# Query root norms kept per token and applied to the attention scores, key root norms spread by one matmul

## What is computed

```python
n = rms_norm(h, attn_norm_w[l])
proj = n @ w_in[l]
aq, ak, av, rq, rk, rv, rg = jnp.split(proj, split_at, axis=-1)
aq = rope(rms_norm(aq.reshape(B, S, ATTN_HEADS, HEAD_DIM), q_norm_w[l]), pos)
ak = rope(rms_norm(ak.reshape(B, S, ATTN_KV_HEADS, HEAD_DIM), k_norm_w[l]), pos)
...
y_attn = windowed_gqa_sink(aq, ak, av, attn_sink[l])
...
def windowed_gqa_sink(q, k, v, sink):
    ...
    s = jnp.einsum('bnqkgd,bnjkd->bnkgqj', qb, kb).astype(jnp.float32) * scale
    s = jnp.where(valid[None, :, None, None], s, NEG_INF)
    m = jnp.maximum(jnp.max(s, axis=-1, keepdims=True), sink_l)
    p = jnp.exp(s - m)
    p = p / (jnp.sum(p, axis=-1, keepdims=True) + jnp.exp(sink_l - m))
```

## Time and profile before

| what | value |
|---|---|
| median of 3 runs | 2899.54 us (2899.49 to 2899.75) |
| the profiled execution's own time | 2900.2 us |
| its span | 2898.4 us |
| mean granted clock of PE | 0.987 |
| DVE, ACT, POOL busy over the span | 1596.1, 902.5, 1333.3 us |
| PE busy from 0 to 72 us | 52.22 us |
| PE busy from 72 to 145 us | 65.04 us |
| PE busy from 145 to 217 us | 72.00 us |

### The profile page before, as it was taken

One profiled execution on the slowest core, in us unless ns is written; L12 is line 12 of the kernel. 1 busy time (PEld: TensorE's weight loads), 2 busy tenths in 40 slices (PEclk: granted clock), 3 DMA queues, 4 the chain that ended last, 5 costly groups with the idle time before them and its releaser, 6 DMA issues. The chain is left out here.

```text
span 2898.4 us, 37077 instructions
## 1 busy us (share of the span) xinstructions
PE 2778.3 (96%) x13968; PEld 2248.7 (78%) x13968; DVE 1596.1 (55%) x2447; ACT 902.5 (31%) x1759; POOL 1333.3 (46%) x1012
## 2 busy tenths in 40 slices
PE   7899989999999999999999899999899999999997
PEld 5677768778888888777766688878777788888886
DVE  5576775485555555542367742133368655555555
ACT  5444422232222222333334510121243332222222
POOL 3323232355666556543222235446614656566663
PEclk9999999999999999999999999999999999999998
DMA  3010101111111111131101011122201111111111
GB/s 123 30 36 30 37 20 73 51 44 51 52 58 59 44 55 51 48 116 37 37 30 38 28 39 51 54 113 66 66 23 44 48 59 55 48 55 52 59 51 66
DMA packets 71378, 151.97 MB, mean 52 GB/s; under 512 B 6449, under 2 KB 29361, under 8 KB 70065
## 3 DMA queue, kind: packets, MB, share of 16 engines
q1 hardware_dynamic: 64256, 123.76, 13.4%
q10 hardware_dynamic: 6960, 26.01, 2.3%
HBM read 141.36 MB, written 8.39 MB: 52 GB/s over the span
## 5 line engine op out<-in xcount | busy, mean ns | idle before, releaser
L612 POOL TENSOR_TENSOR WH<-WRAW,CST 128x512 fp32r<-128x512 f32 x204 | 229.7, 1126 | 895.0 <-PE PS L728 768.7
L726 PE MATMUL PS<-XH,WH 128*128 128x512 f32 x1248 | 512.1, 410 | 3.5 <-DVE XL L2040 2.8
L728 PE MATMUL PS<-XH,WL 128*128 128x512 f32 x1248 | 489.6, 392 | 0.0
L727 PE MATMUL PS<-XL,WH 128*128 128x512 f32 x1248 | 488.9, 392 | 0.0
L637 POOL TENSOR_TENSOR WL<-WRAW,WH 128x512 fp32r<-128x512 f32 x216 | 309.7, 1434 | 273.1 <-ACT WH L1668 272.1
L2460 DVE TENSOR_TENSOR H<-H,PS 128x512 f32<-128x512 f32 x352 | 236.2, 684 | 161.8 <-PE PS L1052 159.4
L726 PEld LDWEIGHTS PS<-XH,WH 128*128 128x128 f32 x1248 | 235.5, 189 | 84.1 <-issue 37.2
L1050 PE MATMUL PS<-HH,WH 128*128 128x512 f32 x704 | 275.8, 392 | 5.3 <-DVE HL L2394 5.3
L614 POOL TENSOR_TENSOR WL<-WRAW,WH 128x512 fp32r<-128x512 f32 x204 | 272.1, 1334 | 16.0
L1668 ACT ACTIVATE WH<-WRAW 128x512 fp32r<-128x512 f32 x204 | 129.0, 632 | 471.6 <-PE PS L1052 383.3
L1051 PE MATMUL PS<-HL,WH 128*128 128x512 f32 x704 | 275.3, 391 | 0.0
(11 more groups left out here) (328 smaller groups left out, 5028.5 us busy)
## 6 DMA issues: line engine op xcount, KB each, us to landing
WRAW<-ws SPq DMA_DIRECT2D x104, 512.0 KB, 3.4
WRAW<-ws SPq DMA_DIRECT2D x176, 256.0 KB, 2.6
RAWX<-ws SPq DMA_DIRECT2D x88, 256.0 KB, 2.6
H<-xT ACTq DMA_DIRECT2D x4, 1024.0 KB, 11.3
H<-xT ACTq DMA_DIRECT2D x2, 2048.0 KB, 9.8
h_spill<-H ACTq DMA_DIRECT2D x1, 4096.0 KB, 12.9
H<-h_spill ACTq DMA_DIRECT2D x4, 1024.0 KB, 8.3
outT<-H ACTq DMA_DIRECT2D x4, 1024.0 KB, 4.4
```

The lines of the kernel that those rows point to most:

```text
L612: pool.tensor_tensor(WH[:, j, c], WRAW[:, j, c], ONES[:, 0:1].to_broadcast((P, 512)), ALU.mult).then_inc(hi_split, 1)
L726: pe.matmul(out, WH[:, j, w], rh(kt), start=(n == 0), stop=False)
L727: pe.matmul(out, WH[:, j, w], rl(kt), start=False, stop=False)
L728: last = pe.matmul(out, WL[:, j, w], rh(kt), start=False, stop=(n == len(kts) - 1))
```

## The change

Four edits. The inverse roots of query heads stay per token in a new tile `RTQ` (128x64), and DVE writes `Q1` without them (a plain add); the roots and the factor 0.125 are applied elsewhere. The mask step is now one multiply-add per head: scores times the query's inverse root of this token, plus the mask. For keys the squares are summed by one matmul with `BD` as weights, so that the sum of a head stands on each of its channels for each of 512 tokens; ACT takes the root of 128x512 into `XX[:, 1024:1536]`, DVE inverts all of it and multiplies it in, with the 0.125. `spread1` and its places in the hook are gone. And `norm_spread(0, 0)` moves from tile 3 to tile 6. The whole diff:

```diff
--- before.py
+++ after.py
@@ -251,7 +251,8 @@
         WH = sb(ctx, "WH", [P, 2, 1024], F32R)
         WL = sb(ctx, "WL", [P, 2, 1024], F32R)
         VEC = sb(ctx, "VEC", [P, NVEC])
-        sb(ctx, "as_the_weights", [P, 40])
+        RTQ = sb(ctx, "RTQ", [P, 64])
+        sb(ctx, "as_the_weights", [P, 104])
         CST = sb(ctx, "CST", [P, NKEEP])
         ACC = sb(ctx, "ACC", [P, 2, HALF])
         SQ = sb(ctx, "SQ", [P, 2, HALF])
@@ -355,7 +356,7 @@
             "r_turned", "r_kz", "r_kv", "r_state", "r_qx", "r_in", "r_si", "r_out", "r_copied"))
         r_sq, r_sum, r_root, r_inv, r_spread, r_norm = map(sem, ("r_sq", "r_sum", "r_root", "r_inv", "r_spread", "r_norm"))
         gate_th, gated, turned_heads, rst_made = map(sem, ("gate_th", "gated", "turned_heads", "rst_made"))
-        head_inv, head_spread = map(sem, ("head_inv", "head_spread"))
+        head_inv = sem("head_inv")
 
 
         prod, w_sum, w_high, w_high0, w_low = map(sem, ("prod", "w_sum", "w_high", "w_high0", "w_low"))
@@ -398,6 +399,10 @@
         def prob(s):
 
             return XX[:, 768 * (s % 2):768 * (s % 2) + 768].rearrange("p (a b) -> p a b", a=2)
+
+        def query_norm(j, b, n):
+
+            return RTQ[:, 16 * j + 2 * b:16 * j + 2 * b + n]
 
 
         RST = [RG[:, 3, half(h)] for h in range(2)]
@@ -854,9 +859,12 @@
                         pe.wait_ge(m_free, nm.n)
                     else:
                         pe.wait_ge(rst_made, 2)
-                    for b in range(4):
-                        sq = XX[:, (g % 2) * HALF + b * P:(g % 2) * HALF + (b + 1) * P]
-                        last = pe.matmul(PS[:, MB, 2 * b:2 * b + 2], sq, BD[:, 0:P:64], start=True, stop=True)
+                    x = XX[:, (g % 2) * HALF:(g % 2 + 1) * HALF]
+                    if kind == "k":
+                        last = pe.matmul(PS[:, MB], BD, x, start=True, stop=True)
+                    else:
+                        for b in range(4):
+                            last = pe.matmul(PS[:, MB, 2 * b:2 * b + 2], x[:, blk(b)], BD[:, 0:P:64], start=True, stop=True)
                     last.then_inc(m_full, 1)
                     nm.n += 1
                 elif kind == "v":
@@ -870,24 +878,12 @@
             def first_norm(h, kt):
                 if (h, kt) == (1, 0):
                     norm_sums(0, 0)
-                if (h, kt) == (1, 3):
+                if (h, kt) == (1, 6):
                     norm_spread(0, 0)
-
-            def spread1(g):
-
-                pe.wait_ge(head_inv, g + 1)
-                if g:
-                    pe.wait_ge(proj_done, g)
-                for b in range(4):
-                    for hh in range(2):
-                        c = 60 + 8 * (g % 2) + 2 * b + hh
-                        last = pe.matmul(PS[64 * hh:64 * hh + 64, OB, blk(b)], STAT[:, c:c + 1].to_broadcast((P, 64)), IDENT,
-                                         start=True, stop=True)
-                last.then_inc(head_spread, 1)
 
             first_units(0, XS_N1, between=first_norm)
             norm_sums(0, 1)
-            done = spreads = 0
+            done = 0
             for g in range(4, 44):
                 u, h = SLOTS1[g]
                 s = g - 12
@@ -895,7 +891,7 @@
                     scores1(s)
 
                 def hook(kt):
-                    nonlocal done, spreads
+                    nonlocal done
                     if kt == 4 and s >= 1:
                         turn1(s - 1)
                     if (g, kt) == (4, 2):
@@ -903,9 +899,6 @@
                     elif done < g - 1 and (kt == 6 if g > 12 else kt in (2, 5)):
                         after1(done)
                         done += 1
-                    elif kt in (4, 7) and spreads < min(done, 10):
-                        spread1(spreads)
-                        spreads += 1
 
                 unit_half(u, h, hook=hook)
                 if s >= 1:
@@ -1526,8 +1519,12 @@
                 if kind in "qk":
                     act.wait_ge(m_full, nm.n + 1)
                     nm.n += 1
-                    act.activation(STAT[:, 60 + 8 * (g % 2):68 + 8 * (g % 2)], PS[:, MB, 0:8], ACT.Sqrt, scale=1.0 / 64,
-                                   bias=v(V_EPS)).then_inc(m_free, 1)
+                    if kind == "q":
+                        dst, src = query_norm(u, 4 * h, 8), PS[:, MB, 0:8]
+                    else:
+                        act.wait_ge(proj_done, PD[g - 1])
+                        dst, src = XX[:, 1024:1536], PS[:, MB]
+                    act.activation(dst, src, ACT.Sqrt, scale=1.0 / 64, bias=v(V_EPS)).then_inc(m_free, 1)
                 elif kind == "v":
                     act.wait_ge(m_full, nm.n + 1)
                     nm.n += 1
@@ -2144,19 +2141,17 @@
                     dve.scalar_tensor_tensor(out=a, in0=a, scalar=scale, in1=ROPE[:, 0, half(h)], op0=ALU.mult,
                                              op1=ALU.mult)
                 link(dve.tensor_tensor(r, r, ROPE[:, 1, half(h)], ALU.mult))
-                if kind in "qk":
-                    stats, rt = STAT[:, 60 + 8 * (g % 2):68 + 8 * (g % 2)], PS[:, OB]
+                if kind == "q":
+                    dve.tensor_tensor(Q1[:, u, half(h)], a, r, ALU.add).then_inc(proj_done, 1)
+                    dve.wait_ge(m_free, g + 1)
+                    dve.reciprocal(query_norm(u, 4 * h, 8), query_norm(u, 4 * h, 8)).then_inc(head_inv, 1)
+                elif kind == "k":
+                    rt = XX[:, 1024:1536]
                     link(dve.tensor_tensor(a, a, r, ALU.add))
                     dve.wait_ge(m_free, g + 1)
-                    dve.reciprocal(stats, stats).then_inc(head_inv, 1)
-                    dve.wait_ge(head_spread, g + 1)
-                    dst = K1[:, half(h)] if kind == "k" else Q1[:, u, half(h)]
-                    if kind == "q":
-
-                        dve.scalar_tensor_tensor(out=dst, in0=a, scalar=0.125, in1=rt, op0=ALU.mult,
-                                                 op1=ALU.mult).then_inc(proj_done, 1)
-                    else:
-                        dve.tensor_tensor(dst, a, rt, ALU.mult).then_inc(proj_done, 1)
+                    link(dve.reciprocal(rt, rt))
+                    dve.scalar_tensor_tensor(out=K1[:, half(h)], in0=a, scalar=0.125, in1=rt, op0=ALU.mult,
+                                             op1=ALU.mult).then_inc(proj_done, 1)
                 else:
                     dst = RK[:, u - U_RK, half(h)] if kind == "r" else RQ[:, u - U_RQ, half(h)]
                     dve.tensor_tensor(dst, a, r, ALU.add).then_inc(proj_done, 1)
@@ -2173,11 +2168,14 @@
                 if s == 0:
                     dve.wait_ge(mask_in, 16)
                     dve.wait_ge(vec_ready, 1)
+                    dve.wait_ge(head_inv, 8)
                 if s >= 2:
                     dve.wait_ge(turned, s - 1)
                 p = prob(s)[:, :, 0:nk]
-                dve.tensor_tensor(p, PS[:, SB:SB + 2, 0:nk], XX[:, off:off + nk].unsqueeze(1).broadcast_to((P, 2, nk)),
-                                  ALU.add).then_inc(masked, 1)
+                for hh in range(2):
+                    ins = dve.scalar_tensor_tensor(out=p[:, hh], in0=PS[:, SB + hh, 0:nk], scalar=query_norm(j, b, 2)[:, hh:hh + 1],
+                                                   in1=XX[:, off:off + nk], op0=ALU.mult, op1=ALU.add)
+                ins.then_inc(masked, 1)
                 dve.wait_ge(masked, s + 1)
                 link(dve.tensor_reduce(stat(s, 0), p, AX.X, ALU.max))
                 sink = v(V_SINK + 2 * j, 2)
```

## The result

The changed kernel takes 2881.57 us (median of 4 runs, 2877.33 to 2884.29) against 2899.57 before (4 runs, 2899.49 to 2899.75): a ratio of 0.9937, interval 0.9919 to 0.9954. It is 18.0 us faster. The forecast had the direction and the path to the first score right. It went wrong behind that: the slow clock that follows the new wait cost more than was taken for it, and the stages behind the scores, which were taken as unchanged, lost time as well. The profiled execution took 2882.12 us, its span 2880.3.

The account below looks back on a forecast made before the run. PE, busy 96% of 2898.4 us, was taken as the bound. First score at 101.0 against 124.43 saves 23.4, rounded 23.5: 2899.5 - 23.5 = 2876.0 us. Own range 2874 to 2878; with two rivals 2871.5 to 2881.

Parts of the forecast that it names:

- The bound and the ring: Before the first scores: the L884 spread holds PE in a ring; without it, 4.8 us of ring against PE's 6.28 per slot.
- Rivals C and E: C: waits move to ACT's square at L859, 9.2 saved, 2890, chance 0.05. E: another ring member, nothing saved, 2899.5, chance 0.02.
- The new waits at head sums: L859 before the scores: PE waits for ACT's turned slot and root, 1.8 us at the fifth sum, 0.6 at the sixth.
- The wait of 0.9 us for the row: PE's wait for ACT's copy of the row stays: 0.9 us, 1.2 with the start of the wait.
- The key sum: One BD matmul against 512 f32 columns replaces four small sums: taken at 1.0 us, 0.4 us more for the two.
- The key chain: From slot 9's end at 84.0: 16.5 us through ACT and DVE, ending at 100.4; PE stands 3.5 us before the first score.
- The price of the slow clock: PE's 3.5 us wait at the first score may bring slow clock: 0 or 1.4 us, 0.5 taken.
- Behind it PE's queue is the same before and after: The first scores, at 124.43 before, end the sum; PE's queue and its pace behind them were taken as unchanged.
- the 23.4 of the working: Saving up to the first score: 101.0 against 124.43, 23.4 us, rounded to 23.5.
- The mask step: Scores stage: two multiply-adds replace one add, 0.15 to 0.25 us more DVE time per step, hidden in waits at L2201; cost 0.
- Rival D: Scores stage: DVE becomes the bound, both mask operations 1.1 us behind POOL; net 12 us slower, 2911, chance 0.03.
- The move: Token-root spread placed 18 matmuls later: PE's wait at L783 goes, some 2.8 us, and unit 2 starts at 39.95.

## Why the prediction was wrong, point by point

**The bound and the ring: right.** The spread held a ring together, and without it PE is the bound. The slots are 6.39 us apart (6.28 forecast), and all waits at L884 are gone. Rivals C and E fall with the openings at 70.93, 77.32 and 83.71, which wait for PE, while PE waits for none of them.

**The new waits at head sums: oversized.** 1.8 and 0.6 us were forecast at the fifth and sixth; 0.34 and 0.34 are listed. The wait of 0.9 us for the row stayed, as said. The key sum was taken at 1.0 us against a head sum's 0.81; slots with it (84.87 to 91.21) last 6.34 us, the query ones 6.38, so it costs nothing more.

**The key chain: right.** Both reciprocals took 3.35 us, as the row of the kernel before had it. The repeat count of 8 that the Trainium skill states (VectorE: DVE Perf Modes, First, the fixed hardware budget) would by the prediction's estimate have given 4.27; by that rule the first score would be later, and the trace disagrees. The delay of the second product by POOL was 0.75 us (0.5 taken of 0 to 1.1). PE's wait was listed at 4.1 us (3.5 + 0.5 forecast), and the first score came at 100.5. The forecast's 101.0 holds 0.5 us of slow clock that came behind the score and not ahead of it; without that it says 100.5, too. (Two of its sums are off by 0.1: the end of slot 11 adds up to 96.6 and not 96.7, the end of the chain to 100.5 and not 100.4.) One thing the forecast didn't look at: POOL also delayed the three operations of the first keys ahead of the first reciprocal, by 2.2 us together (1.09, 1.76 and 1.41 us where the same ones took 0.74, 0.68 and 0.69 in the slot ahead). It cost nothing, since DVE was through at 88.53 and ACT's root, which the reciprocal needs as well, at 88.57; but there was no slack left.

**The price of the slow clock: this is the first step that failed.** The text said: "a wait of 3.5 us may bring the slow clock: 0 [...] or 1.4 [...]; I take 0.5". Measured: 1.5 to 2.9 us in five profiles of five with that wait, 3.0 in slot 12 of the first, and nothing in the two in which the wait was filled. Both ends of my bound came from waits of 2.5 us, which are shorter than the one I was pricing, so the upper end was no bound. With the mean of 2.2 in place of 0.5 the forecast is 2877.7, with the 2.9 of the profiled execution 2878.4, so this step alone doesn't account for the miss.

**"Behind it PE's queue is the same before and after": true, and not enough; this is the second step that failed.** It put the change behind the scores at nothing. The same queue took 1.7 us more in retention and projection and 1.4 more in the middle in the first pair. The range had no room for that. Retention and projection scatter by 8 us over all kernels here, while the first three runs of the kernel before agreed within 0.3 us and let me think that nothing scatters. The whole account, against the 23.4 of the working: 0.5 more ahead of the first score, 2.9 less in the scores, 1.7 and 1.4 less behind, 0.2 more at the end, which is 18.1. Of the 3.1 us behind the scores it is not shown that the change causes them; that stays open. Chance has its part in the number, too: in the job in which the changed kernel was 23 us faster than before, the forecast of 23.5 would have looked right with the same wrong price in it.

**The mask step: right.** 2 x 0.613 less the overlap: 27.4 us for 24 steps are 1.14 each against 0.957, 0.19 more (0.15 to 0.25 forecast), hidden. But DVE's waits for PE's values, which were to shrink by 0.2 per step, went from 50.7 to 48.1 us over the scores, 0.08 per step. Rival D is out: no instance took over 0.620 us, though POOL ran beside many. That agrees with what the Trainium skill states (SBUF — State Buffer, SBUF: two separate sides), that of DVE's operations only those with two SBUF inputs, or in a two-port mode, contend with GpSimd; the key product with two SBUF inputs was delayed by 0.75 us.

**The move: right**, 2.8 us forecast, 2.7 and 2.8 measured the two ways.

## What to carry to other kernels

When a change takes PE out of a ring, look for the first place where a long operation of the new chain is read whole, and ask what part of it is read first: waiting for half the keys only was worth 5 us by the stretches and 6 to 7 by the times, beside the 18 of the whole change. Price a new wait of PE together with the clock behind it, from waits at least as long, and treat the short ones as no evidence. And before giving a range, ask which stretches behind the edit have PE idle often; here these scattered by 8 us, with the clock, though the first runs agreed within 0.3 us.

## What the runs showed of the hardware that was not expected

The clock after a wait: after 4.1 us of standing, slow in five profiles of five; after 2.1 us or 0.3 us with the same start, not slow in three of three; after 2.45 to 2.68 us, slow or not by the instance. The two profiles of before, the move alone and the spread moved back hold nine such waits at spreads; behind five of them the spread took 1.83 to 2.07 us, behind the other four 1.09 to 1.16. Useless matmuls in a wait keep the clock up, and in the stretch they pay exactly what the clock had cost; in the whole time the gain could not be told from the scatter beside the changed kernel. Finally, an f32 matmul of 128x512 with a fixed weight holds the queue no longer than four of two columns with changing weights: 6.34 against 6.38 us per slot.
